# A two-layer decoder trunk in float32 on one core: the sum of expert rows joined with sliding attention, the mixer's output product joined with cross attention

## The reference

```python
for l in range(2):
    h = rmsnorm(x, norm_mix[l])
    x = x + (hybrid_mixer(h, ...) if l == 0 else swa_mixer(h, ...))      # ends in "o @ w_out (+ b_out)"
    h = rmsnorm(x, norm_xattn[l])
    q = (h @ xattn_w_q[l]).reshape(B, S, 4, 128)
    p = softmax(einsum('bshd,bmhd->bhsm', q, mem_k) * 128 ** -0.5)
    x = x + einsum('bhsm,bmhd->bshd', p, mem_v).reshape(B, S, 512) @ xattn_w_o[l]
    x = x + hier_moe(rmsnorm(x, norm_ffn[l]), ...)                       # two expert rows per token, weighted and summed
return rmsnorm(x, final_norm)
```

## Time and profile before

| | us |
|---|---|
| median of 3 runs | 2734.83 |
| lowest and highest | 2733.21, 2737.17 |
| profiled execution | 2735.03 |
| its span | 2733.2 |
| PE busy | 2476.5 |
| DVE busy | 857.1 |
| ACT busy | 410.3 |
| POOL busy | 286.5 |

### The profile page before, as it was taken

The page is one execution under the profiler, slowest core; times in us unless marked ns, Lnnn a source line. Parts: engine busy times, 40 slices in busy tenths (PEclk is TensorE's granted clock), DMA queues, the critical chain, the costliest instruction groups (busy, mean ns, idle before and its releaser), DMA issues. The chain is left out here.

```text
span 2733.2 us, 28240 instructions
## 1 busy us (share of the span) xinstructions
PE 2476.5 (91%) x9824; PEld 1302.9 (48%) x9824; DVE 857.1 (31%) x1507; ACT 410.3 (15%) x1003; POOL 286.5 (10%) x303
## 2 busy tenths in 40 slices
PE   6999999898995999999994999989996899999992
PEld 4667676644642444444442464634553344444440
DVE  3344352642243111111115273665136111111114
ACT  2122121211310000000001051411221000000001
POOL 0000000320000000000004030351000000000003
PEclk9999999999997999999996999999998899999996
DMA  6010101105136999999994110110023899999996
GB/s 208 24 31 15 46 16 61 38 1 231 53 146 231 389 403 403 403 403 403 403 381 158 32 24 24 69 39 0 31 72 143 310 401 404 403 404 403 403 393 237
DMA packets 204297, 563.07 MB, mean 206 GB/s; under 512 B 33104, under 2 KB 70864, under 8 KB 204112
## 3 DMA queue, kind: packets, MB, share of 16 engines
q1 hardware_dynamic: 182208, 493.64, 47.4%
q0 software_dynamic: 12000, 42.74, 4.5%
q10 hardware_dynamic: 10032, 25.96, 2.4%
HBM read 506.19 MB, written 55.05 MB: 205 GB/s over the span
## 5 line engine op out<-in xcount | busy, mean ns | idle before, releaser
L1965 PE MATMUL pair<-W,yT 128*128 128x512 f32 x1056 | 465.4, 599 | 0.0
L1965 PEld LDWEIGHTS pair<-W,yT 128*128 128x128 f32 x1056 | 199.2, 191 | 241.2 <-issue 238.8
L1978 PE MATMUL pO<-hT,yT 128*64 128x512 f32 x1056 | 233.9, 595 | 13.0 <-ACT yT L2071 12.0
L2007 PE MATMUL pair<-W,yT 128*128 128x512 f32 x528 | 232.3, 593 | 0.0
L808 PE MATMUL pU<-hT,W 128*128 128x256 f32 x768 | 174.7, 380 | 5.2 <-DVE W L950 2.4
L2112 DVE TENSOR_TENSOR tmp<-probT,pair 128x512 f32<-128x512 f32 x33 | 22.7, 688 | 460.1 <-ACT probT L2050 460.1
L808 PEld LDWEIGHTS pU<-hT,W 128*128 128x128 f32 x768 | 142.2, 190 | 26.2 <-issue 5.0
L2007 PEld LDWEIGHTS pair<-W,yT 128*128 128x128 f32 x528 | 97.7, 190 | 112.1 <-issue 112.1
L1978 PEld LDWEIGHTS pO<-hT,yT 128*64 128x64 f32 x1056 | 75.4, 137 | 150.3 <-issue 150.3
L1133 PE MATMUL pair<-hT,W 128*128 128x512 f32 x320 | 139.8, 599 | 3.3 <-SPq L85 3.3
L2116 DVE TENSOR_TENSOR tmp<-probT,pO 64x512 f32<-64x512 f32 x33 | 22.4, 679 | 359.0 <-ACT probT L2054 359.0
(11 more groups left out here) (313 smaller groups left out, 2946.6 us busy)
## 6 DMA issues: line engine op xcount, KB each, us to landing
W<-in_moe_w_gate_up_dram SPq DMA_DIRECT2D x132, 1024.0 KB, 12.7
hT<-in_moe_w_gate_up_dram SPq DMA_DIRECT2D x132, 1024.0 KB, 16.1
W<-in_moe_w_down_dram SPq DMA_DIRECT2D x66, 1024.0 KB, 16.2
yT<-in_moe_w_down_dram SPq DMA_DIRECT2D x66, 1024.0 KB, 13.4
y_rows<-prob ACTq DMA_DIRECT2D x33, 512.0 KB, 6.7
y_rows<-qk SPq DMA_DIRECT2D x31, 512.0 KB, 14.7
W<-in_hyb_w_in_dram SPq DMA_DIRECT2D x24, 512.0 KB, 3.8
y_rows<-yT ACTq DMA_DIRECT2D x66, 128.0 KB, 6.3
```

Source lines behind the costliest of these rows:

```text
L1965: ins = nc.tensor.matmul(A[:, 512 * h:512 * h + 512], xt_l[:, k, :], gu_l[:, k, 512 * h:512 * h + 512], start=(k == 0), stop=(k == KD - 1))
L1978: ins = nc.tensor.matmul(pO[HS * (1 - h):HS * (1 - h) + HS, :], xt_s[:, k, :], gu_s[:, k, 512 * h:512 * h + 512], start=(k == 0), stop=(k ...
L2007: ins = nc.tensor.matmul(B[:, 512 * h:512 * h + 512], ht_l[:, f, :], dn_l[:, f, 512 * h:512 * h + 512], start=(f == 0), stop=(f == 3))
```

## The change

1. The phase of the sum of expert rows and the sliding attention become one phase. PE projects b = 0, 1 and 2 for one block of 128 tokens (`project_block`) behind the transposes of the next block. The projections b = 3 and 4 and the V product, and all of turn 2, stay whole.
2. The results of the projections rotate over three places: A, B, and pO with pU; V goes to pO and pU. ACT and DVE therefore evict them in halves of 512 columns.
3. The loop over j is written out, so that waits are on constants.
4. SP gives the starting credits at the head of the joint phase, and issues the first weights only when the first block is summed (`x_done`).
5. Each mixer output product and the cross attention behind it become one phase. Query chunk 0 is computed in two halves of four matmuls: the first right behind the last product, then the transposes of block 6, the second half, the transposes of block 7, and scores 0. Chunks 1 and 2 follow. SP's output weights and zero rows wait for all products in place of the barrier.

The diff, without the many lines that only change their indent or turn a block into a returned function:

```diff
 def stream(name, nblk, src, gain, feed, ..., rest=None, window=None):
     @block.sync
+        if window:
+            give_credits(sp)
+            sp.wait_ge(x_done, 1)
         ...
+        if window:
+            window_sync(sp)            # gpsimd, scalar, vector alike at the end of their lists
     @block.tensor
                 elif not final:
                     transposes(c)
+                    if window and c:
+                        project_block(pe, c - 1)
     ...
+        if window:
+            pe.wait_ge(ev_done, 2 * nblk)
+            project_block(pe, nblk - 1)
+            window_tensor(pe)

-def strassen_stream(name, gain, w_ready, bias=None, preload=None):
+def strassen_stream(name, gain, w_ready, rest, bias=None, preload=None):
     ...
-        transposes(NB - 2)
-        transposes(NB - 1)
+        pe.wait_ge(ev_done, 8)
+        pe.wait_ge(added, read_at[(NPR * NT - 5) // NPR, ORDER[(NPR * NT - 5) % NPR]])
+        rest_tensor(pe, [lambda: transposes(NB - 2), lambda: transposes(NB - 1)],
+                    [(added, v)], (ev_done, 2 * NB))

 def window_attention():
+    place = [(A[:, 0:512], A[:, 512:1024]), (B[:, 0:512], B[:, 512:1024]), (pO[:, :], pU[:, :]),
+             (A[:, 0:512], A[:, 512:1024]), (B[:, 0:512], B[:, 512:1024])]
+    def project_block(pe, c):
+        for b in range(3):
+            if c == 0:
+                pe.wait_ge(w_loaded[b], 32)
+            for k in range(KD):
+                ins = nc.tensor.matmul(place[b][c // 4][:, (c % 4) * P:(c % 4) * P + P], slot[b][:, k, :],
+                                       hT[:, k, c * P:(c + 1) * P], start=(k == 0), stop=(k == KD - 1))
+            if c == NB - 1:
+                ins.then_inc(product[b], 1)
     def project(j, b):
         pe.wait_ge(w_loaded[b], j * (16 if b == K_ else 32))
-        if b >= 2:
-            pe.wait_ge(raw_done, j * 5 + b - 1)
+        if b == 2:
+            pe.wait_ge(o_stored, j * NS)
+        if b >= 3:
+            pe.wait_ge(raw_done, j * 5 + b - 2)
     ...
-    with pe.Fori(1, 3) as j:
+    for j in (1, 2):
-        for b in range(V_):
+        for b in range(3 if j == 1 else 0, V_):
             project(j, b)
     ...
         scores(j, 0)
-        pe.wait_ge(v_added, j + 1)
         scores(j, 1)
+        pe.wait_ge(v_added, j + 1)

 def cross_attention(l):
-    load_out_matrix(xattn_w_o[l], 1 + 2 * l)(sp)
+    def on_sync(sp, products):
+        sp.wait_ge(*products)
+        load_out_matrix(xattn_w_o[l], 1 + 2 * l)(sp)
     ...
-    project_chunk(0)
-    project_chunk(1)
-    scores(0)
-    project_chunk(2)
-    scores(1)
+    for h in range(2):
+        for k in range(4 * h, 4 * h + 4):
+            ins = nc.tensor.matmul(pU[:, :], slot[0][:, k, :], hT[:, k, 0:512],
+                                   start=(k == 0), stop=(k == KD - 1))
+        if h:
+            ins.then_inc(chunk, 1)
+        last_transposes[h]()
+    for need in all_added:
+        pe.wait_ge(*need)
+    scores(0)
+    pe.wait_ge(*all_evacuated)
+    project_chunk(1)
+    project_chunk(2)
+    scores(1)
```

More of the change, by code:

```diff
@@ L312, in _ @@
                         rest.scalar(act)
+                    if window:
+                        window_scalar(act)
                 @block.vector
@@ new lines, in on_sync, with double_keys @@
+            def on_sync(sp):
+                def double_keys(j):
+                    sp.wait_ge(rope_step, j * 20 + 20)
+                    sp.dma_start(Kd[0][64:128, :], Kd[0][0:64, :]).then_inc(k_doubled, 16)
+                    sp.dma_start(Kd[1][0:64, :], Kd[1][64:128, :]).then_inc(k_doubled, 16)
+                for j, b in [(j, b) for j in (1, 2) for b in range(NBLK)][3:]:
+                    if (j, b) == (2, 2):
+                        double_keys(1)
+                    sp.wait_ge(product[(b + 3) % 6], j + 1 if b >= 3 else j)
+                    load_window(sp, j, b)
+                    if b == V_:
+                        sp.wait_ge(turned, j * NS)
+                        sp.dma_start(vbias, vectors[:, (j - 1) * P + V_VB:j * P + V_VB]
+                                     ).then_inc(vb_loaded, 16)
+                double_keys(2)
+                load_out_matrix(swa_w_out[0], 2)(sp)
@@ new lines, in on_sync, with on_gpsimd @@
+            def on_sync(sp, products):
+                sp.wait_ge(*products)
+                load_out_matrix(xattn_w_o[l], 1 + 2 * l)(sp)
+                if l == 0:
+                    sp.wait_ge(zeroed, 1)
+                    for r0, r1 in unwritten:
+                        sp.dma_start(y_dram[r0:r1, :], zero_rows[0:r1 - r0, :]).then_inc(cleared, 16)
+            def on_gpsimd(pool, products):
+                if l == 0:
+                    pool.wait_ge(*products)
+                    nc.gpsimd.memset(zero_rows, 0.0).then_inc(zeroed, 1)
@@ new lines, in on_scalar, with keep_queries, exps, store @@
+            def on_scalar(act):
+                def keep_queries(s):
+                    act.wait_ge(chunk, s + 1)
+                    wait(act, scored, s - 3)
+                    nc.scalar.activation(Q[s % 4], pU[:, :], ACT.Copy, scale=float(P) ** -0.5).then_inc(q_ready, 1)
+                def exps(s):
+                    act.wait_ge(maxed, s + 1)
+                    wait(act, turned1, s - 1)
+                    wait(act, inverted, s - 1)
+                    for r in range(4):
+                        ins = nc.scalar.activation(PR[s % 2][:, r, :], SC[s % 2][:, r, :], ACT.Exp,
+                                                   bias=nmax[:, s % 2, r:r + 1],
+                                                   accum_out=psum_[:, s % 2, r:r + 1])
+                    ins.then_inc(exped, 1)
+                def store(s):
+                    act.wait_ge(o_turned, s + 1)
+                    nc.scalar.activation(yT[:, s // 2, 512 * (s % 2):512 * (s % 2) + 512], pU[:, :],
+                                         ACT.Copy).then_inc(o_stored, 1)
+                keep_queries(0)
+                keep_queries(1)
+                exps(0)
+                keep_queries(2)
+                exps(1)
+                for s in range(NS):
+                    act.wait_ge(turned0, s + 1)
+                    wait(act, weighed, s)
+                    nc.scalar.activation(probT[:, 0:512], C[:, 0:512], ACT.Copy).then_inc(copied0, 1)
+                    if s:
+                        store(s - 1)
+                    if s + 2 < NS:
+                        exps(s + 2)
+                    if s + 3 < NS:
+                        keep_queries(s + 3)
+                store(NS - 1)
@@ L1507, in build @@
+            return on_sync, on_gpsimd, on_tensor, on_scalar, on_vector
         NL = NG + NE
```

589 lines of the change are left out of this document (265 added, 324 removed).

## The result

The changed kernel takes 2707.49 us (median of 4 runs, 2707.38 to 2708.22) against 2736.0 us of the kernel before, measured beside it; the ratio is 0.9897 with an interval of [0.988, 0.9914]. That is faster by 1%, but only two thirds of what was forecast: the profiled span falls from 2733.2 to 2705.6 us, by 27.6 instead of 42.0.

The account below looks back on a forecast made before the run. TensorE, busy 91% of the span, was taken as the bound, so time could come only from its idle or half-clock stretches. Savings of 20.9, 10.8 and 10.3, together 42.0 us, from 2735.0 gave 2693 us, range 2690 to 2697.

Parts of the forecast that it names:

- Parts 2 and 3: Mixer output product joined with cross attention: 26.5 us from last product to probabilities' transposes; 10.8 us saved in layer 0, 10.3 in layer 1.
- rival 4: Cross borders: TensorE waits again for block 7's norm, with only 0.8 us of slack; 2701 us, chance 6%.
- The mixed stage at full clock: Expert-row sum with first three projections: block products between transposes run at full clock, 6.23 us a round.
- rival 1: Expert-row sum with projections: the clock never rises, block products run at half clock; 2741 us, chance 4%.
- The rule that the prediction sets against its forecast: Products thinner than 512 need ordering without waits or padding; by it, 128-column block products between transposes run at 1.2 GHz.
- The exposed reload: Before the fourth projection: slot 0's weights load no longer hides behind projections; a wait of 0.5 us.
- rival 3: Before the fourth projection: slot 0's reload takes 9.9 us, TensorE waits 6 us and starts at low clock; 2701 us, 6%.
- The first weights: Six loads moved behind the first summed block: expected by 1470 to 1475, cost nothing, up to 7 us if late.
- Rival 2: Block 0: first weights come late, slot 2 at 1484, block 0 ends near 1487; +7, 2700 us, chance 10%.
- The written-out loop: Sliding attention's loop over j unrolled: takes counters out of waits in rows standing back to back; gain nothing.

Follow-up runs that it names:

- the last experiment: The kernel before with only ScalarE's loop over the two steps of the sliding attention written out; 2735.58 us, ratio 1.0005.
- the cross border alone: The kernel before with only the mixer's output product and cross attention joined, in both layers; 2717.22 us, ratio 0.9936.
- the two repairs: The changed kernel with first weights issued without waiting for the first summed block, and a one-column exponential ahead of the two steps; 2698.41 us, ratio 0.987.
- table early: The changed kernel with one exponential of one column ahead of the two steps, so its table loads early; 2702.67 us, ratio 0.9882.
- window alone: The changed kernel with the borders of output product and cross attention as in the kernel before; 2725.99 us, ratio 0.9967.
- weights early: The changed kernel without the wait for the first summed block ahead of the first weights; 2700.26 us, ratio 0.9872.

## Why the prediction was wrong

- **Parts 2 and 3, right.** Forecast 10.8 and 10.3, measured 10.4 and 9.9; each border is 0.4 us longer than 26.5. The clock holds, as forecast, and rival 4 (the slack of 0.8 us) did not come.
- **The mixed stage at full clock, right.** Rounds of 6.24 us at 1.00; rival 1 is out. The rule that the prediction sets against its forecast speaks of waits between thin products, and from the third round on there were none. The exposed reload was forecast at 0.5 us and took 0.83, so rival 3 is out too.
- **The first weights, wrong: the step that failed.** "Cost: nothing, with up to 7 us if this cover fails." The reason given was that "the eight gathers ahead of them" are 4.2 MB and "nearly through". From the first issue (1461.4) to the last weights (1470 to 1475) the prediction allows 9 to 14 us. The changed kernel takes 23.0, and four more kernels with the same 256-byte rows take 23.6 to 26.3, issued early or late. So the time of the six loads beside gathers is the term that was sized wrong, and the change moved its start from 0.7 us ahead of the first gather's issue to 7.7 us behind it. I had put 10.8 us for eight gathers and 7.5 us of the engines' time for the loads, and counted the gathers ahead of the loads and not those behind: six of the sixteen were issued before the first load, ten after it. The row length is a shown part of the time (18.1 us in rows of 512 bytes); that the later gathers are another is argued from their bytes, as no run takes them away. Rival 2 had it, with slot 2 at 1484 and the end of block 0 near 1487; on the time axis of the kernel before, the changed kernel has 1483.9 and 1487.4. Its chance of 10% was too small, since the earlier trace rows already had the loads at 9.9 us under this load against 3.5 without, and block 0 asked for all three slots within 7 us. Its price of 7 left out the next round, partly at half clock (1.2 us more), and 0.3 at the reload.
- **The written-out loop, wrong.** "The unrolled loop takes counters out of the waits ... nothing." It moved a table load into the one place of the window where TensorE waits for ScalarE. That costs 1.27 us, and 2.4 with the clock of this execution against the kernel before. I had looked at that table load, but only where it stood before. The trace agrees with the Trainium skill, ScalarE activation tables: per-element evaluation and per-set limits, "Table sets in the compiler and the runtime": table loads are placed block by block of the program. With the loop the load stood at its head, ahead of the first eviction; written out, it moved to the first exponential, in the last experiment too. That a written-out loop stops being a block of its own is my reading and is not shown.
- **What was won unforeseen.** The first gathers land 1.7 us sooner without the weights beside them. The early issue gives 1.6 of this back, so 7.0 of its 8.6 us would be left, and 6.2 were measured.
- **What stays open.** The first gather of layer 1's experts. With the same instructions around it, TensorE's wait for it is 9.64 us in the kernel before, 9.72 with ScalarE's loop written out and 10.04 with the cross border alone, but 11.59, 11.21, 11.59, 11.84, 11.76 and 11.60 in the six kernels with the joined window. The first rows of these lines in before and after:

```profile
2126.10 1.97 PE L1947 MATMUL pair<-ident,yT 128*128 128x128 f32 x8 [9.64 <-DMA yT<-h_rows,icol]
```
```profile
2098.00 1.97 PE L1999 MATMUL pair<-ident,yT 128*128 128x128 f32 x8 [11.59 <-DMA yT<-h_rows,icol]
```

It goes with the joined window, half a millisecond earlier, and no run here tells why. With the two repairs the time is 2698.4 us; of the 5.4 us that remain to the forecast, this wait is about 2 and the borders 0.8. The rest is not traced; executions of the kernel before alone lie up to 8.5 us apart.

## What to carry to other kernels

When a load is moved, take its time from a trace that has it beside the same traffic, from the first issue to the last landing, and price it by its rows as well as by its bytes. When a loop is written out, look where the table load of each non-linear function goes, and put a one-column call ahead if it lands in front of a waiting engine. A border between two stages can be closed where the next stage has products that don't need the last blocks of the one before.

## What the hardware showed that I had not expected

- Six loads of 256 KB kept their issuing queue for 16.74 us in rows of 256 bytes and for 5.37 us in rows of 512 bytes, beside the same gathers; the last was usable 23.0 and 18.1 us after the first issue. The Trainium skill, DMA: Bandwidth & Descriptors, "Specifications", asks for 512 bytes or more for the full rate; the traces agree in direction.
- Waits in a stretch that starts at half clock did not have one price. With waits of 2.91 and 1.84 us in block 0 the round behind had a granted clock of 0.83. With 1.90, 1.33 and 0.80 us (table early) and with 1.83, 1.14 and 3.58 us (window alone) it had 1.00, though the last idled longer. With a single wait of 0.84 us (weights early) block 0 itself had 0.79 instead of 0.60.
